# A second product in place of a transposition: the transposed factor of a triangular inverse in a chunked recurrence

## The reference

```
def wkv_scan(r, w, k, v, kk, a, s0, reverse):
    def step(S, inp):
        r_t, w_t, k_t, v_t, kk_t, a_t = inp
        sa = jnp.einsum("bhvk,bhk->bhv", S, kk_t)
        S = (S * w_t[:, :, None, :]
             - sa[..., None] * (kk_t * a_t)[:, :, None, :]
             + v_t[..., None] * k_t[:, :, None, :])
        return S, jnp.einsum("bhvk,bhk->bhv", S, r_t)
    s_fin, o = lax.scan(step, s0, xs, reverse=reverse)
    return jnp.moveaxis(o, 0, 1), s_fin
```

## Time and profile before

| | us |
|---|---|
| median of 3 runs | 2525.03 |
| lowest, highest | 2523.11, 2528.29 |
| span of the profiled execution | 2537.7 |
| TensorE busy in it | 2172.6 (86%) |
| weight loads | 1625.2 (64%) |
| DVE, ACT, POOL busy | 1354.0, 1152.3, 681.8 |

### The profile page before, as it was taken

The page is one execution under the profiler, slowest core; times in us unless marked ns, Lnnn a source line. Parts: engine busy times, 40 slices in busy tenths (PEclk is TensorE's granted clock), DMA queues, the critical chain, the costliest instruction groups (busy, mean ns, idle before and its releaser), DMA issues.

```text
span 2537.7 us, 59405 instructions
## 1 busy us (share of the span) xinstructions
PE 2172.6 (86%) x25764; PEld 1625.2 (64%) x25764; DVE 1354.0 (53%) x2324; ACT 1152.3 (45%) x1933; POOL 681.8 (27%) x412
## 2 busy tenths in 40 slices
PE   8799999288888888887789999996888987898888
PEld 2587777067766767676667666663666665666666
DVE  1357878434444455454345666664356663466752
ACT  2466767233333334343335454543355553355552
POOL 0334443200001011011433222222443332433332
PEclk9899999589998899998989999997999998999998
DMA  7215453652332222312313111111222221222222
GB/s 259 71 59 170 132 159 117 179 147 78 100 105 75 68 63 51 78 43 71 135 56 108 51 50 54 55 42 43 90 75 83 67 67 66 67 79 76 63 67 67
DMA packets 156163, 221.37 MB, mean 87 GB/s; under 512 B 84480, under 2 KB 109312, under 8 KB 155136
## 3 DMA queue, kind: packets, MB, share of 16 engines
q1 hardware_dynamic: 144800, 174.32, 22.4%
q0 software_dynamic: 9952, 40.11, 5.2%
q10 hardware_dynamic: 1152, 3.15, 0.3%
HBM read 164.84 MB, written 42.21 MB: 82 GB/s over the span
## 4 chain that ended last, share of the span: by engine, by line
PE 59%; DVE 15%; ACT 11%; issue 8%; POOL 4%; DMA 2%; SPq 0%; ACTq 0%; DVEq 0%; POOLq 0%
PE ps L257 8%; PE ps L259 7%; PE ps L258 7%; PE ps L1337 3%; PE ps L543 3%; PE ps L1327 2%; PE ps L1352 2%; PE ps L2257 2%; PE ps L396 2%; PE ps L2794 2%; PE ps L2217 1%; PE ps L2771 1%; PE ps L1202 1%; ACT p L2277 1%; DVE s L921 1%
## 5 line engine op out<-in xcount | busy, mean ns | idle before, releaser
L242 POOL TENSOR_TENSOR wbl<-wb,wbh 128x1024 fp32r<-128x1024 f32 x128 | 309.4, 2418 | 661.3 <-ACT wbh L237 657.5
L257 PE MATMUL ps<-hTh,wah 128*128 128x512 f32 (+1 forms) x512 | 180.6, 353 | 17.3 <-POOL wal L242 10.8
L257 PE MATMUL ps<-hT2h,wbh 128*128 128x512 f32 x416 | 180.2, 433 | 10.7 <-POOL wbl L242 10.5
L258 PE MATMUL ps<-hTl,wah 128*128 128x512 f32 (+1 forms) x512 | 174.9, 342 | 0.0
L259 PE MATMUL ps<-hTh,wal 128*128 128x512 f32 (+1 forms) x512 | 174.7, 341 | 0.0
L257 PE MATMUL ps<-hT1h,wbh 128*128 128x512 f32 (+1 forms) x432 | 169.0, 391 | 3.1 <-POOL hT1l L2398 3.1
L344 POOL TENSOR_TENSOR ro<-ro 128x256 f32<-128x256 f32 (+1 forms) x12 | 11.9, 993 | 586.7 <-DVE ro L328 586.7
L237 ACT ACTIVATE wbh<-wb 128x1024 fp32r<-128x1024 f32 x128 | 134.6, 1052 | 69.5 <-PE ps L1936 43.5
L259 PE MATMUL ps<-hT2h,wbl 128*128 128x512 f32 x416 | 164.5, 395 | 0.0
L258 PE MATMUL ps<-hT2l,wbh 128*128 128x512 f32 x416 | 163.9, 394 | 0.0
L242 POOL TENSOR_TENSOR wal<-wa,wah 128x1024 fp32r<-128x1024 f32 x34 | 102.2, 3008 | 219.2 <-ACT wah L237 219.2
(11 more groups left out here) (410 smaller groups left out, 5612.6 us busy)
## 6 DMA issues: line engine op xcount, KB each, us to landing
wb<-in_w_in SPq DMA_DIRECT2D x56, 512.0 KB, 3.5
s_str_dram<-s POOLq DMA_DIRECT2D x48, 576.0 KB, 8.7
wm<-in_ada SPq DMA_DIRECT2D x48, 512.0 KB, 4.5
bkv<-s_str_dram SPq DMA_DIRECT2D x96, 192.0 KB, 3.3
wa<-in_rw_in SPq DMA_DIRECT2D x34, 512.0 KB, 4.4
wb<-in_da_in SPq DMA_DIRECT2D x32, 512.0 KB, 3.4
ARI<-s_str_dram SPq DMA_DIRECT2D x96, 128.0 KB, 3.4
wb<-in_w_out SPq DMA_DIRECT2D x16, 512.0 KB, 3.5
```

Of the source, the lines that this page charges most:

```text
L242: e.tensor_tensor(self.lo[:, n % 2], self.raw[:, n % 3], self.hi[:, n % 2].bitcast(F32), ALU.subtract).then_inc(self.K.s.w_lo, 1)
L257: e.matmul(z, wh[:, k, :], hi[:, k, a:b], start=k == 0, stop=False)
L258: e.matmul(z, wh[:, k, :], lo[:, k, a:b], start=False, stop=False)
```

## The change

At levels 1 to 4 `pe_update` gets a second set of 16 products, with Y as first operand and E as second: it gives the transposed factor of the new D, in columns 256 to 511. The four transposes ahead of `pe_level` go. ACT then copies both halves at once (128 by 1024 elements instead of twice 128 by 512), behind the update, so there is one ACT copy for each level instead of two. `pe_level` waits for this copy; `pe_update` and DVE's masked copy no longer wait for ACT. The counts of `iv_a` fall from 12 to 8 for a unit. The number of steps, and so the interleaving, is the same. The new L1334 is the old L1337, the new L1349 the old L1352; L1355 is the second set.

```diff
-        if l > 1:
-            for d, h in QUADS:
-                e.transpose(ps[:, x + h, 256 + 128 * d:384 + 128 * d], D[:, h, 128 * d:128 * d + 128], K.ident)
...
                 m = e.matmul(ps[half(c), x + h, blk64(2 * d + q)], *z, start=True, stop=True)
+        if l < 5:
+
+            for d, c in QUADS:
+                for h, q in TILES:
+                    E = self.E1[half(h), 2 * d + q, c, :] if l == 1 else old[half(h), q, blk64(4 + 2 * d + c)]
+                    m = e.matmul(ps[half(q), x + h, blk64(4 + 2 * d + c)], self.Y[half(h), l - 1, c, blk64(2 * d + q)], E,
+                                 start=True, stop=True)
         m.then_inc(self.iv[u % 2][0], 1)
...
         for l in range(1, 5):
             e.wait_ge(*self.iv_at(u, v=l + 1))
-            e.wait_ge(*self.iv_at(u, a=2 * l - 1))
             self.pe_update(e, u, l)
             yield
-            e.wait_ge(*self.iv_at(u, a=2 * l))
+            e.wait_ge(*self.iv_at(u, a=l + 1))
             self.pe_level(e, u, l + 1, "jp"[l % 2])
...
         for l in range(1, 5):
             e.wait_ge(*self.iv_at(u, mm=2 * l + 2))
-            e.activation(self.DE[:, u % 2, 1 - l % 2, :, 0:256], banks[:, :, 0:256], ACT.Copy).then_inc(a, 1)
+            e.activation(self.DE[:, u % 2, 1 - l % 2], banks, ACT.Copy).then_inc(a, 1)
             yield
-            e.wait_ge(*self.iv_at(u, mm=2 * l + 3))
-            e.activation(self.DE[:, u % 2, 1 - l % 2, :, 256:512], banks[:, :, 256:512], ACT.Copy).then_inc(a, 1)
             yield
...
             e.wait_ge(*self.iv_at(u, mm=2 * l + 1))
-            if l > 1:
-
-                e.wait_ge(*self.iv_at(u, a=2 * l - 1))
             if u:
                 e.wait_ge(*self.iv_at(u - 1, mm=2 * l + 2))
             e.copy_predicated(self.Y[:, l - 1], twice(self.mY[l - 1]), banks[:, :, 0:256]).then_inc(v, 1)
```

More of the change, by code:

```diff
@@ L1314, in iv_at @@
         if a is not None:
-            return A, 12 * (u // 2) + a
+            return A, 8 * (u // 2) + a
         if v is not None:
@@ L1359, in pe_invert @@
         if u >= 2:
-            e.wait_ge(*self.iv_at(u - 2, a=12))
+            e.wait_ge(*self.iv_at(u - 2, a=8))
             e.wait_ge(*self.iv_at(u - 2, v=8))
@@ L1382, in pe_invert @@
         e.wait_ge(*self.iv_at(u, v=6))
-        e.wait_ge(*self.iv_at(u, a=9))
         self.pe_update(e, u, 5)
         yield
-        e.wait_ge(*self.iv_at(u, a=10))
+        e.wait_ge(*self.iv_at(u, a=6))
         e.wait_ge(*self.use[self.x_use(u)])
@@ L1395, in pe_invert @@
         yield
-        e.wait_ge(*self.iv_at(u, a=11))
+        e.wait_ge(*self.iv_at(u, a=7))
         for d, c in QUADS:
@@ L1497, in dve_invert @@
         yield
-        e.wait_ge(*self.iv_at(u, a=12))
+        e.wait_ge(*self.iv_at(u, a=8))
         if u:
@@ L1780, in turned_in @@
         for u in (22, 23):
-            e.wait_ge(*self.scan.iv_at(u, a=12))
+            e.wait_ge(*self.scan.iv_at(u, a=8))
             e.wait_ge(*self.scan.iv_at(u, v=8))
```

## The result

| | median us | lowest to highest | runs |
|---|---|---|---|
| before | 2526.66 | 2523.11 to 2532.49 | 4 |
| after | 2569.14 | 2562.53 to 2575.13 | 4 |

The changed kernel is slower: ratio 1.0161, 95% interval 1.0135 to 1.0187, or 42 us (34 to 47). The forecast was 2559 us, slower, with a range of 2516 to 2588. The profiled execution of after took 2575.13 us with a span of 2573.3; between the two profiled spans lie 35.6 us.

What follows compares the result with a forecast made beforehand. TensorE's work was taken as the bound, with instruction supply beside it. Work and waits summed to -27 us (-27 -10 +10); with supply, 1.9 us in 18 units gave +34 on 2525: 2559 us, range 2516 to 2588.

Steps and rivals of the forecast that it cites:

- The bound: TensorE in the recurrence: 256-instruction blocks arrive no sooner than about 3.8 us apart, 4.7 us while the recurrence's fetches run.
- The count: Profile after: 28452 loads and as many matmuls, 225 instruction packets, 96 ACT copies fewer.
- The price of 1.9 us a unit in 18 units: Recurrence: 2.5 us more in the instruction-dense part, -0.6 us in the thin part, by 18 units: +34 us.
- six units with a readout: Recurrence units where TensorE waits behind a readout; a block comes in meanwhile, so they were counted at nothing.
- the dense part: Second part of a unit, 645 loads in 18.53 us: 84 loads more, priced at 2.5 us a unit.
- TensorE's work, -27 us: Levels 1 to 4: transposes removed, 16 small products added; 0.28 us less a level over 96, before instruction supply.
- DVE's wait, -10 us: Update's weight loads waiting 19.4 us for DVE's masked copy: 10 us of it goes as DVE stops waiting for ACT.
- the new copy's wait, +10 us: Next level waits for the whole ACT copy: about 0.4 us lost once a unit, 10 us over 24.
- rival 3: Larger copy's wait uncovered at two or three levels a unit, plus supply as forecast: 2580 to 2600 us; chance 0.12.
- Rival 1: Recurrence: supply does not grow into a bound, TensorE's work decides: -27 us, 2498 us (2477 to 2520); chance 0.12.
- Rival 2: Recurrence: gain and supply cancel, the extra block costing 1 us a unit instead of 3.4; 2522 us; chance 0.09.
- Rival 4: Every unit, readouts too, pays its full 3.4 us and TensorE's gain is eaten: +82 us, 2607 us; chance 0.05.

Runs made afterwards that it cites:

- the series in isolation: Kernel before plus three series of 64-row products without waits behind its last product (64 columns, 256 columns, 64 columns under DMA load): 2699.12 us, one execution.
- the padding pair: Kernel before plus unread columns written at levels 1 to 4: by 14 products of 8 columns, 2608.21 us; by one product of 256 columns, 2557.43 us.
- the single-level runs: Kernel before with the second set and one wide copy at one level only: level 4, 2553.94 us; level 3, 2550.72 us.

## Why the prediction was right

**The bound.** The reading that TensorE's program comes in blocks of 256 instructions at about 3.8 us, later under DMA load, is shown: by the series in isolation (3.47 to 4.02 us, under load up to 4.84), by after (3.75, 4.57), and by the padding pair, where about the same busy time of the matmuls in 56 instead of 4 instructions costs 51 us more. That it is what the change costs is shown by the run with transposes in the products' place (the same busy time and the same waits, and the cost is gone). The 4.7 us under load are the upper end: in isolation the mean was 4.2.

**The count.** 28452 loads, 225 packets, ACT 96 copies fewer: exact.

**The size.** The price of 1.9 us a unit in 18 units, 34 us, stands against 32 between the profiled recurrences and 42 (34 to 47) between the medians. The mechanism was right, the term a little small. That six units with a readout pay next to nothing held: they grew by 3.7 us together. But one of them is among the first nine units and five among the last fourteen, so 1.9 us for each of the others makes 15 and 17 us; measured are 19.4 and 12.7, which is 2.4 us for an early unit without a readout and 1.0 for a late one, and single units moved by -5.4 to +6.8. The price was worked out from late units, for which it was twice too high. That the total came so near is in part luck. And the harm was put into the dense part alone, with -0.6 us in the thin one; the single-level runs show level 4, in the thin part, costing as much as level 3.

**TensorE's work, -27 us.** The loads run for 6.0 us less and PE is busy for 15.8 less in the stretch, but the weight loads are busy for 11.8 more (440.85 and 452.69). That the saving vanishes behind the supply was the forecast; the run without the second set shows a second reason, as 42 us less of running loads gave 14 in that stretch and 8 in the median: 18 us more of waiting for DVE and ACT, so time saved ahead of such a wait can come back as waiting.

**DVE's wait, -10 us, and the new copy's wait, +10 us.** The first was wrong in sign: 19.4 us became 25.3. The added instructions are not the reason, since the same wait is 24.9 us without the second set and 26.3 with transposes in its place; why it grew is open. The second was 16.0 us, 11 more than the transposes' wait for ACT, and under the 20 that would have spoken for rival 3. The run with transposes in the products' place has both and costs nothing in all, as other idle time fell by as much. The prediction had +10 and -10 here and so zero; that this came out is right in the sum only.

**The rivals.** Rival 1 (the supply is no bound, 2498 us), which is also the Trainium skill's second half-sentence, falls with the isolated series and the padding pair. Rival 2 did not hold for the change. Rival 3 falls with the run just named. Rival 4 would have been +82 us.

No variant that computes the full result beat the kernel before.

## What to carry to other kernels

Count instructions as well as time: where TensorE runs small float32 products back to back, 256 instructions are issued in 1.95 us and the next 256 are there after 3.5 to 4.8, so replacing four transposes (8 instructions) by sixteen small products (64) can lose although the busy time of the matmuls falls. The signs in a profile are idle time of weight loads put down to "issue" inside a group of equal products, the same number of loads apart. And price a saving by the wait behind it: in the run without the second set, the time gained was a third of the work's length or less.

## What the hardware showed beyond that

- The instruction packet of a block is recorded about 1.1 us after the block before it begins (the 60 in the fifth slice from 2547.1), and the block itself begins 2.6 us later still, at 2550.89. What fills these 2.6 us no row shows.
- 14 products of 8 columns keep PE busy for 0.66 us (63.1 us over 96 levels), one product of 256 columns for 0.63. Fewer columns in a small product saved almost nothing: 16 products of 64 columns are 0.77 us (73.5 over 96), which is 0.67 for 14.
- Moving the block boundaries by half a block, with 32 small products in an idle stretch ahead of the recurrence, cost the kernel before 0.33% (0.17 to 0.49).
